# A hybrid decoder layer on one core: the tile of meta and decode tokens packed from 40 rows to 24

## The chip, the core and the metric

The kernel runs on one core of a Trainium2 chip. The metric is the device time in microseconds (us) of one execution. The engines are TensorE (PE, with its weight loads shown apart as PEld), VectorE (DVE), ScalarE (ACT), GpSimd (POOL) and SyncE (SP), which here only issues transfers. Each engine works through its own list in order and waits on semaphores for the others.

## The reference, cut to what matters

One layer of a decoder for 512 prompt tokens, 16 learned meta tokens in front of them and 8 decode tokens (one for each of 8 sequences). All is float32.

```python
p = rms_norm(x, g) @ w_in              # 1024 -> 3080: mq mk mv mo gates dq dk dv
# mLSTM heads (4) on mq, mk, mv, gates; differential attention heads (4) on dq, dk, dv;
# decode tokens: paged keys and values, and a kept state C, n, m
hm = rms_norm(h_m, g_m) * sigmoid(mo)
ha = rms_norm(a, g_da) * (1.0 - lam_init)
x = x + concatenate([hm, ha]) @ w_out  # 1024 -> 1024
# MoE: best of 4 groups, best 2 of its 8 experts (256 wide), SwiGLU, y summed with gates
for e in range(32):
    y += gates[:, e:e+1] * ((silu(h @ w_gate[e]) * (h @ w_up[e])) @ w_down[e])
```

## The kernel before, in words

Tokens lie in five tiles: tiles 0 to 3 hold 128 prompt tokens each, tile 4 (T4) the small rest. In T4 rows 0 to 15 are the meta tokens, rows 16 to 31 are padding and rows 32 to 39 are the decode tokens (S0 = 32, N4 = 40), so that each kind begins at a partition from which engines may start.

A list, `ORDER`, made by `schedule()`, sets the order in which all engines handle the items; each engine runs through the list and takes the part that is its own. Up to the experts it goes like this:

- The six projection blocks dv, dq, dk, mqk, mv, mo (512 columns each). An item `acc` (with `pre` as its first half) is a product for 128 or 512 prompt tokens; it runs 8 steps over the input dimension (L2054 where the result is stored by feature, L2057 where by token). An item `small` is the same block for T4 (L2071): the 40 rows of T4 are the weights of the array, the block's columns stream through. Since 40 rows fill less than half of the array's columns, the 512 columns of the block are cut in two halves of 256, whose results go to partitions 0 to 39 and 64 to 103 of one bank: two column groups of 64. ACT copies each half out (L1077).
- `qk`, `tp`, `pv` (attention of one tile and head: scores, turned weights, values) are woven between the products of blocks mqk, mv and mo, so that PE has work while DVE and ACT do the softmax. The decode tokens' attention is done beside it: `decscore`, `decsm`, `dect`, `decmix`, `decmix2` (L2010: values of four tokens at a time into four column groups of 32), `decsel`.
- The mLSTM: `decay`, `mqk_s`, `mpa`, `mpb` for four heads, `mdec1` to `mdec3` for the kept state of the decode tokens. `mdec1` needs the state C (`WS<-in_state_C`, L690) and the decode queries spread to all partitions (`DVt<-dec_mq`, L694), both brought by SP. Beside it `sig` items on DVE turn the gate mo of one half of a tile into a sigmoid times a gain (L1435, L1436, L1438).
- The output projection: `wa` (attention half, L2277) and `wo` (mLSTM half), each for tile and half of 512 columns, for T4 both halves together (L2281) in two column groups of 64. DVE adds the result to X (L1650, and for T4 also L1653). Norm (`hs`, `on`), turning (`ot`, `rt`), router (`logit`) lie around it.
- `rank`, `invert`, `order` find which rows go to which of 16 pairs of experts.

Then 17 turns over pairs of experts follow: gather of rows, gate and up (L2328), down (L2345), scatter. The 96 weight matrices of 1 MB are loaded by SP into 20 places; those for the first pairs are loaded as soon as a place is free, items 2 to 10 after `ot` of tile 0, for which SP waits until the product `wa` of T4 is done.

```python
ins = v.tensor_tensor(xs, xs, PS[b][0:n, :], ALU.add)          # wa, wo: L1650
...
drained(sp, ("pv",) + UNITS[-1], "p")                          # SP, item mdec1
```

## Time and profile before

| | us |
|---|---|
| median of 3 runs | 671.25 |
| lowest, highest | 669.18, 678.52 |
| the profiled execution, its own time | 677.67 |
| its span, first to last instruction | 675.8 |
| mean granted TensorE clock in it | 0.96 |

PE is busy for 91% of the span. The table of stretches below gives the busy time of each engine in one stretch, its instructions in brackets, then the granted clock of TensorE (1.00 is 2.4 GHz, 0.50 is 1.2 GHz), the busy share of the DMA engines and GB/s. In a timeline a row is: start in us, length in us, engine, line, operation, what it writes and reads, the size of the array used (rows*columns) or of the tiles, and in square brackets how long the engine stood still before it and who ended that. A float32 product counts as two instructions. The chain of waits is the chain of work that ended last, in order of time: start, length, what.

### The profile page before, as it was taken

What the parts mean: (1) busy time and instruction counts of PE and PEld (TensorE: products, weight loads), DVE (VectorE), ACT (ScalarE), POOL (GpSimd) and SP (SyncE); (2) the same over time, 40 slices, a digit from 0 to 9 for tenths busy, and PEclk for the clock granted to TensorE, in tenths of its full rate; (3) what the DMA queues carried; (4) which work ended last, traced back from release to release, by engine and by line L of the source; (5) the groups of instructions that cost most, each with busy time, mean ns of one, the idle gap of its engine ahead of it and who ended that gap; (6) DMA issues with size and microseconds to landing.
All of it is one profiled execution on the core that took longest, in us unless ns stands there. A gap on an engine that the chain in (4) does not pass through costs nothing.

```text
span 675.8 us, 8726 instructions
## 1 busy us (share of the span) xinstructions
PE 613.0 (91%) x3213; PEld 330.0 (49%) x3213; DVE 282.8 (42%) x637; ACT 139.7 (21%) x410; POOL 118.5 (18%) x206
## 2 busy tenths in 40 slices
PE   4999999799899999999989993899999996999792
PEld 2444444445544555555544562665555553555430
DVE  2320048443343434457969957714121221112066
ACT  2210132233332355221031110101001000100012
POOL 2341006220012011101032101111231111120013
PEclk9999999799999999999999896899999998999897
DMA  9636156750603030031759999599999999999993
GB/s 286 205 101 191 29 191 180 256 167 0 250 19 107 1 125 0 1 75 53 221 164 424 316 342 362 223 415 420 400 418 419 419 421 421 422 419 419 417 379 135
DMA packets 59409, 165.77 MB, mean 245 GB/s; under 512 B 18345, under 2 KB 27866, under 8 KB 46694
## 3 DMA queue, kind: packets, MB, share of 16 engines
q1 hardware_dynamic: 49590, 147.97, 57.6%
q0 software_dynamic: 7552, 17.19, 7.9%
q8 instruction: 27, 0.44, 0.3%
q10 hardware_dynamic: 2224, 0.04, 0.2%
q14 instruction: 16, 0.13, 0.1%
HBM read 150.88 MB, written 23.34 MB: 258 GB/s over the span
## 4 chain that ended last, share of the span: by engine, by line
PE 74%; DMA 13%; DVE 6%; ACT 2%; issue 2%; another core or an unknown queue 2%; POOL 0%; SPq 0%; POOLq 0%; DVEq 0%; ACTq 0%
PE bank L2054 12%; PE bank L2057 11%; PE bank L2277 9%; PE scores L2345 8%; PE bank_t L2328 6%; PE bank_p L2328 6%; DMA WS<-in_w_down_e 4%; DMA XHT<-in_w_down_e 4%; PE bank_t L2071 3%; PE bank L2318 2%; DMA WS<-in_w_in 2%; PE bank_p L2180 1%; PE scores L2197 1%; PE bank_t L2299 1%
## 5 line engine op out<-in xcount | busy, mean ns | idle before, releaser
L2057 PE MATMUL bank<-WS,XHT 128*128 128x512 f32 x192 | 89.1, 611 | 3.1 <-DMA WS<-in_w_in 2.6
L2054 PE MATMUL bank<-XHT,WS 128*128 128x512 f32 x192 | 86.5, 606 | 1.4 <-PE bank_t L2071 1.4
L2054 PEld LDWEIGHTS bank<-XHT,WS 128*128 128x128 f32 x192 | 36.3, 194 | 44.6 <-issue 44.3
L2057 PEld LDWEIGHTS bank<-WS,XHT 128*128 128x128 f32 x192 | 35.4, 193 | 44.7 <-issue 41.4
L2328 PE MATMUL bank_p<-WS,XHT 128*64 128x256 f32 x256 | 43.3, 381 | 1.5 <-DMA XHT<-in_w_up_e 1.3
L987 POOL DMA_INDIRECT out_rows<-MVA,slot_ids x15 | 15.1, 1008 | 153.1 <-DVE MVA L1851 150.4
L2328 PE MATMUL bank_t<-WS,XHT 128*64 128x256 f32 x224 | 39.4, 381 | 0.2 <-DVE XHT L1834 0.2
L874 POOL TENSOR_SCALAR rr<-ss 128x1 f32<-128x1 f32 (+3 forms) x25 | 7.3, 293 | 150.3 <-ACT XHT L1249 44.1
L2328 PEld LDWEIGHTS bank_p<-WS,XHT 128*64 128x64 f32 x256 | 26.8, 137 | 13.9 <-DMA XHT<-in_w_up_e 1.7
L2345 PE MATMUL scores<-WS,FT 128*64 128x512 f32 x72 | 28.0, 672 | 5.6 <-DMA WS<-in_w_down_e 5.6
L1851 DVE COPY MVA<-scores 128x512 f32<-128x512 f32 x16 | 11.1, 692 | 49.8 <-PE scores L2345 49.8
L2277 PE MATMUL bank<-WS,XHT 128*128 128x512 f32 x64 | 30.4, 623 | 0.0
L1586 DVE TENSOR_TENSOR scores<-scores,maskneg 128x256 f32<-128x256 f32 (+1 forms) x20 | 7.7, 383 | 54.3 <-PE scores L2151 49.2
L2277 PE MATMUL bank<-WS,FT 128*128 128x512 f32 x64 | 29.6, 605 | 0.1
L2328 PEld LDWEIGHTS bank_t<-WS,XHT 128*64 128x64 f32 x224 | 23.9, 137 | 11.2 <-issue 0.3
L1926 DVE TENSOR_TENSOR MVA<-DVt,bank_p 128x256 f32<-128x256 f32 x9 | 3.8, 421 | 59.6 <-ACT DVt L1292 59.6
L2328 PE MATMUL bank_p<-XHT 128*64 128x256 f32 x160 | 28.7, 381 | 0.0
L2328 PE MATMUL bank_t<-XHT 128*64 128x256 f32 x160 | 28.6, 381 | 0.0
L2318 PE MATMUL bank<-ident,DVt 128*128 128x128 f32 x136 | 20.5, 296 | 8.5 <-DMA DVt<-tok_rows,slot_ids 8.5
L915 POOL DMA_INDIRECT MO<-in_cache_k,pages x16 | 16.2, 1010 | 67.8 <-DVE before_mix L1540 50.4
L1077 ACT ACTIVATE MVA<-scores 128x512 f32<-128x512 f32 x18 | 10.6, 597 | 84.0 <-PE scores L2345 84.0
L1926 DVE TENSOR_TENSOR MVA<-DVt,bank_t 128x256 f32<-128x256 f32 x8 | 3.4, 421 | 52.6 <-ACT DVt L1292 52.6
(482 smaller groups left out, 1059.0 us busy)
## 6 DMA issues: line engine op xcount, KB each, us to landing
WS<-in_w_gate_e SPq DMA_DIRECT2D x16, 1024.0 KB, 8.8
WS<-in_w_up_e SPq DMA_DIRECT2D x14, 1024.0 KB
WS<-in_w_down_e SPq DMA_DIRECT2D x14, 1024.0 KB, 18.1
WS<-in_w_in SPq DMA_DIRECT2D x6, 2048.0 KB, 10.8
XHT<-in_w_up_e SPq DMA_DIRECT2D x10, 1024.0 KB
XHT<-in_w_down_e SPq DMA_DIRECT2D x9, 1024.0 KB, 21.4
XHT<-in_w_gate_e SPq DMA_DIRECT2D x8, 1024.0 KB, 30.3
FT<-in_w_up_e SPq DMA_DIRECT2D x6, 1024.0 KB
```

The costliest lines, as they stand in the source:

```text
L915: pool.indirect_dma_start(dst, None, cache[0].rearrange("n t h d -> (n t) (h d)"), bass.IndirectOffsetOnAxis(ap=pages[:, b * NPAGES + p:b ...
L987: pool.indirect_dma_start(end_rows if i in ENDING else out_rows, bass.IndirectOffsetOnAxis(ap=slot_ids[:, c, 1:2].bitcast(u32), axis=0), Y ...
L1077: return act.activation(dst, src, ACT.Copy, scale=scale)
L1586: link(v.tensor_tensor(diag, diag, maskneg[0:n, None, 0:n].to_broadcast([n, 2, n]), ALU.add))
L1851: v.tensor_copy(YO[s][:, 512:1024], Sps[:, 0, 512:1024]).then_inc(y1, 1)
L2054: mm = pe.matmul(PS[r][:, :], w[:, k, 128 * m:128 * (m + 1)], hT[:, k, 0:512], start=(k == 0), stop=(k == KC - 1))
L2057: mm = pe.matmul(PS[r][:, :], hT[:, k, 128 * m:128 * (m + 1)], w[:, k, :], start=(k == 0), stop=(k == KC - 1))
L2071: mm = pe.matmul(PS[r][64 * u:64 * u + N4, 0:256], hT[:, k, 512:TOK], w[:, k, 256 * u:256 * u + 256], start=(k == 0), stop=(k == KC - 1))
L2277: mm = pe.matmul(PS[b][0:n, :], rows[:, k, col(j):col(j) + n], blkslot[(6 + half) % 3][:, first + k, :], start=(k == 0), stop=(k == 3))
L2318: mm = pe.transpose(bank[k // 4][:, 128 * (k % 4):128 * (k % 4) + 128], src[:, k:D:KC], ident[:, :])
L2328: mm = pe.matmul(gu[64 * u:64 * u + 64, DE * g:DE * g + DE], rows[:, k, 64 * u:64 * u + 64], weights[kind, u][:, k, :], start=(k == 0), st ...
L2345: mm = pe.matmul(Sps[64 * u:64 * u + 64, 0, 512 * half:512 * half + 512], act_t[:, f, 64 * u:64 * u + 64], weights["down", u][:, f, 512 * ...
```

## The change

T4 is packed to 24 rows: the meta tokens in rows 0 to 15 and the decode tokens in rows 16 to 23 (SX = 16, NX = 24). With at most 32 rows a product of T4 fits a column group of 32. The `small` items of dv, dq, mqk, mv and mo now run in four column groups of 32, each over 128 of the block's columns; that of dk (the decode keys) stays in two groups of 64 over 256 columns. `wa` and `wo` of T4 run in four groups over 256 of the 1024 output columns each.

The part of the work that DVE, ACT and POOL do on decode tokens alone (rows 32 to 39) stays at those partitions. So five transfers issued by SP copy rows 16 to 23 of DVt, MQ4, MK, MVA and MO to rows 32 to 39, and `turned_rows` puts the turned rows back beside each other. The copy of MO needs the finished `sig` of T4, so the `sig` items come in the order of tiles 0, 1, T4, 2, 3; two more of them lie in the stretch of `mpa` 1 and `mqk_s` 2, two fewer in that of `wo` 2.

```diff
 TOK = SEQ + N4
+
+
+SX = NMETA
+NX = SX + NDEC
+ROWS = SEQ + NX
...
 def nrows(j):
+    return 128 if j < NT else NX
+
+
+def mixed_rows(j):
     return 128 if j < NT else N4
 
...
-    sig = iter([("sig", j, half) for j in range(NTILES) for half in range(2)])
+    sig = iter([("sig", j, half) for j in (0, 1, T4, 2, 3) for half in range(2)])
     gate = lambda: [next(sig)]
     norm = lambda kind: [(kind, j) for j in outer]
     order += [("decay", 0)] + more() + [("tp",) + prev, ("mqk_s", 0)] + more() + [("pv",) + prev] + norm("hsa")
     order += [("decay", 1), ("mpa", 0)] + gate() + more() + [("mqk_s", 1)] + norm("ona") + more() + [("mpb", 0), ("decay", 2)]
-    order += norm("oa") + gate() + more() + [("mpa", 1)] + gate() + more() + [("mqk_s", 2)] + gate() + more()
+    order += norm("oa") + gate() + gate() + more() + [("mpa", 1)] + gate() + gate() + more() + [("mqk_s", 2)] + gate() + more()
     order += [("mpb", 1), ("decay", 3), ("mdec1",)] + more() + [("mpa", 2)] + gate() + more() + [("mqk_s", 3), ("wsk",)] + more()
...
-        order += gate() if j == 2 else []
...
-        order += [("mdec3", 2), ("state",)] if j == 1 else gate() if j == 2 else []
+        order += [("mdec3", 2), ("state",)] if j == 1 else []
...
+def small_groups(b):
+
+    return 2 if b == "dk" else 4
...
+                        sp.dma_start(DVt[S0:N4, T4, :], DVt[SX:NX, T4, :]).then_inc(v_out, 16)
...
-                        sp.dma_start(dec_mq, MQ4[S0:N4]).then_inc(dm_out, 16)
-                        sp.dma_start(dec_mk, MK[S0:N4, T4, :]).then_inc(dm_out, 16)
+                        sp.dma_start(dec_mq, MQ4[SX:NX]).then_inc(dm_out, 16)
+                        sp.dma_start(dec_mk, MK[SX:NX, T4, :]).then_inc(dm_out, 16)
+                        sp.dma_start(MQ4[S0:N4], MQ4[SX:NX]).then_inc(dm_out, 16)
+                        sp.dma_start(MK[S0:N4, T4, :], MK[SX:NX, T4, :]).then_inc(dm_out, 16)
+                    elif item[1] == "mv":
+                        sp.dma_start(MVA[S0:N4, T4, :, 0:DV], MVA[SX:NX, T4, :, 0:DV]).then_inc(dm_out, 16)
+                elif item == ("sig", T4, 1):
+                    sp.wait_ge(mo_gated, 1)
+                    sp.wait_ge(dm_out, 16 * 5)
+                    sp.dma_start(MO[S0:N4, T4, :], MO[SX:NX, T4, :]).then_inc(dm_out, 16)
...
-                    sp.wait_ge(dm_out, 32)
+                    sp.wait_ge(dm_out, 16 * 5)
...
+            def turned_rows(dst, src, j):
+
+                src = src.rearrange("p (k t) -> p k t", t=128)
+                if j < NT:
+                    return copy(dst[:, 0:4, col(j):col(j) + 128], src)
+                copy(dst[:, 0:4, col(j):col(j) + NMETA], src[:, :, 0:NMETA])
+                return copy(dst[:, 0:4, col(j) + SX:col(j) + NX], src[:, :, S0:N4])
+
...
-                    for u in range(2):
-                        src = PS[r][64 * u:64 * u + N4, 0:256]
-                        cols = slice(256 * u, 256 * u + 256)
+                    groups = small_groups(b)
+                    for u in range(groups):
+                        src = PS[r][128 // groups * u:128 // groups * u + NX, 0:512 // groups]
+                        cols = slice(512 // groups * u, 512 // groups * (u + 1))
                         if b == "dq":
-                            ins = copy(tokst[0][0:N4, cols], src, DQ ** -0.5)
+                            ins = copy(tokst[0][0:NX, cols], src, DQ ** -0.5)
                         elif b == "dk":
-                            ins = copy(tokst[1][0:N4, cols], src)
+                            ins = copy(tokst[1][0:NX, cols], src)
                         elif b == "mqk":
-                            ins = copy(MK[0:N4, T4, :], src, DQ ** -0.5) if u else copy(MQ4, src)
+                            ins = (copy(MQ4[0:NX, cols], src) if u < 2 else
+                                   copy(MK[0:NX, T4, 128 * (u - 2):128 * (u - 1)], src, DQ ** -0.5))
                         elif b == "dv":
-                            ins = copy(DVt[0:N4, T4, cols], src)
...
+                    dve.wait_ge(dm_out, 16 * 5)
...
+                    if item == ("sig", T4, 1):
+                        v.nop().then_inc(mo_gated, 1)
...
+                    dve.wait_ge(v_out, 16 * 7)
...
+                        if j == T4:
+                            dve.wait_ge(dm_out, 16 * 6)
...
-                    xs = X[0:n, j, 512 * half:512 * half + 512]
-                    ins = v.tensor_tensor(xs, xs, PS[b][0:n, :], ALU.add)
+                    parts = [(slice(512 * half, 512 * half + 512), PS[b][0:n, :])]
                     if j == T4:
-                        xs = X[0:n, j, 512:1024]
-                        ins = v.tensor_tensor(xs, xs, PS[b][64:64 + n, :], ALU.add)
+                        parts = [(slice(256 * u, 256 * u + 256), PS[b][32 * u:32 * u + n, 0:256]) for u in range(4)]
+                    for c, product in parts:
+                        ins = v.tensor_tensor(X[0:n, j, c], X[0:n, j, c], product, ALU.add)
                     ins.then_inc(freed[b], 1)
...
+                    groups = small_groups(b)
+                    rows, cols = 128 // groups, 512 // groups
                     for k in range(KC):
-                        for u in range(2):
-                            mm = pe.matmul(PS[r][64 * u:64 * u + N4, 0:256], hT[:, k, 512:TOK],
-                                           w[:, k, 256 * u:256 * u + 256], start=(k == 0), stop=(k == KC - 1))
+                        for u in range(groups):
+                            mm = pe.matmul(PS[r][rows * u:rows * u + NX, 0:cols], hT[:, k, 512:ROWS],
+                                           w[:, k, cols * u:cols * u + cols], start=(k == 0), stop=(k == KC - 1))
...
-                        for u in range(2):
-                            mm = pe.matmul(PS[b][64 * u:64 * u + n, :], rows[:, k, 512:TOK], blkslot[(6 + u) % 3][:, first + k, :],
+                        for u in range(4):
+                            mm = pe.matmul(PS[b][32 * u:32 * u + n, 0:256], rows[:, k, 512:ROWS],
+                                           blkslot[(6 + u // 2) % 3][:, first + k, 256 * (u % 2):256 * (u % 2) + 256],
                                            start=(k == 0), stop=(k == 3))
```

DVE, from the end of item `mpa` of head 1 to the beginning of `mpb` of head 1, before (L1435, L1436, L1438 are one `sig` item, L1650 adds a product `wa` to X, L1601 to L1605 multiply scores):

```order
L1622 TENSOR_TENSOR XHT<-bank_t,den 128x3x128 [waits dve_step]
L1435 TENSOR_SCALAR MO<-MO 128x256 [waits freed_a1,freed_t]
L1436 RECIPROCAL MO<-MO 128x256 [waits dve_step]
L1438 TENSOR_TENSOR MO<-MO,head_gains 128x256 [waits dve_step]
L1650 TENSOR_TENSOR XHT<-XHT,bank 128x512 [waits filled_a0,dve_step]
L1601 TENSOR_TENSOR WS<-WS,scores 128x896 [waits filled_Sa,decay_masked]
...
L1435 TENSOR_SCALAR MO<-MO 128x256 [waits freed_a1]
```

and in the changed program (L1469, L1470, L1472 are the `sig` item, L1692 is the addition, L1638 the scores):

```order
L1659 TENSOR_TENSOR XHT<-bank_t,den 128x3x128 [waits dve_step]
L1469 TENSOR_SCALAR MO<-MO 128x256 [waits freed_a1,freed_t]
L1470 RECIPROCAL MO<-MO 128x256 [waits dve_step]
L1472 TENSOR_TENSOR MO<-MO,head_gains 128x256 [waits dve_step]
L1469 TENSOR_SCALAR MO<-MO 24x256 [waits freed_a0,dve_step]
L1470 RECIPROCAL MO<-MO 24x256 [waits dve_step]
L1472 TENSOR_TENSOR MO<-MO,head_gains 24x256 [waits dve_step]
L1692 TENSOR_TENSOR XHT<-XHT,bank 128x512 [waits filled_a0,dve_step]
L1638 TENSOR_TENSOR WS<-WS,scores 128x896 [waits filled_Sa,decay_masked]
...
L1469 TENSOR_SCALAR MO<-MO 24x256 [waits freed_a0]
```

Between the end of `mpa` 1 and the scores there are two `sig` items where there was one, and both `sig` items of T4 now stand here; the other half of tile 1 stands ahead of `mpa` 1, right behind the last item of tile 0.

SP, from the load of the last weight block to the spreading of the decode queries, before:

```order
L599 DMA WS<-in_w_out 128x8x512 [waits block_used]
L690 DMA WS<-in_state_C 128x32x64 [waits block_used,freed_a0,freed_t]
L694 DMA DVt<-dec_mq 128x2048 [waits v_out,freed_p,dm_out]
L697 DMA dec_w<-dr 8x4 [waits dw_made]
L698 DMA dec_w<-dr 8x4
```

and in the changed program:

```order
L612 DMA WS<-in_w_out 128x8x512 [waits block_used]
L678 DMA MVA<-MVA 8x4x128 [waits freed_t]
L682 DMA MO<-MO 8x512 [waits dm_out,mo_gated,freed_a0]
L711 DMA WS<-in_state_C 128x32x64 [waits block_used]
L715 DMA DVt<-dec_mq 128x2048 [waits v_out,freed_p,dm_out]
L718 DMA dec_w<-dr 8x4 [waits dw_made]
```

The copy of MO, which waits for the last `sig` item of T4 on DVE (`mo_gated`), stands ahead of the two transfers that `mdec1` on DVE waits for.

## Rows read from the trace of the kernel before

**Rows 1.** Page, part 1: busy us, share of the span and instructions.
```profile
PE 613.0 (91%) x3213; PEld 330.0 (49%) x3213; DVE 282.8 (42%) x637; ACT 139.7 (21%) x410; POOL 118.5 (18%) x206
```
**Rows 2.** Table of stretches: busy time by engine, clock, DMA share, GB/s.
```profile
126.00:136.00 10.00, 9.14 (x37) 5.15 (x35) 1.88 (x12) 4.00 (x12) 0.17 (x1) 0.66 0.72 271
...
293.00:350.00 57.00, 56.57 (x226) 29.17 (x226) 43.57 (x102) 10.26 (x41) 6.83 (x15) 1.00 0.46 133
...
413.00:440.00 27.00, 16.50 (x131) 12.10 (x133) 19.30 (x69) 2.58 (x7) 4.23 (x4) 0.74 0.69 275
440.00:540.00 100.00, 100.00 (x748) 56.95 (x746) 23.49 (x56) 10.04 (x24) 21.02 (x26) 1.00 1.02 415
```
**Rows 3.** Chain of waits: start, length, what.
```profile
213.15 2.03 PE bank_p L2010 x16
...
346.83 3.59 PE bank L2281 x16
...
353.21 0.66 PE scores L2260 x4
```
**Rows 4.** Timeline of PE in `decmix2`, four column groups of 32.
```profile
213.08 0.63 PE L2010 MATMUL bank_p<-MO,Wd 128*32 128x512 f32 x2
...
213.53 0.61 PE L2010 MATMUL bank_p<-MO,Wd 128*32 128x512 f32 x2
```
**Rows 5.** Timeline of PE: two runs of short products, then `small` of mo.
```profile
86.25 0.74 PE L2037 MATMUL bank_p<-XHT,wg 128*36 128x40 f32 x16
...
292.91 3.65 PE L2071 MATMUL bank<-WS,XHT 128*40 128x256 f32 x32
...
410.90 0.70 PE L1999 MATMUL bank_t<-MO 128*64 128x8 bf16 x20 [1.74 <-DVE MO L1728]
```
**Rows 6.** Timeline around `small` of dq (ACT) and of mqk.
```profile
81.06 0.77 ACT L1077 ACTIVATE XHT<-bank_t 40x256 f32<-40x256 f32 x2 [3.00 <-PE bank_t L2071]
...
158.44 0.25 ACT L1077 ACTIVATE WS<-scores 16x128 f32<-16x128 f32 x1
...
166.84 0.37 DVE L1594 SCALAR_TENSOR_TENSOR WS<-WS,sums 128x144 f32<-128x144 f32 x1
...
168.82 0.27 PE L2161 MATMUL scores<-ident,WS 128*16 128x128 f32 x1
```
**Rows 7.** Timeline of DVE from `mpb` 0 to `wo` of T4.
```profile
294.20 0.29 DVE L1435 TENSOR_SCALAR MO<-MO 128x256 f32<-128x256 f32 x1
...
296.32 0.43 DVE L1438 TENSOR_TENSOR MO<-MO,head_gains 128x256 f32<-128x256 f32 x1
300.20 0.16 DVE L1618 SCALAR_TENSOR_TENSOR den<-bank_t,RC 128x3 f32<-128x3 f32 x1 [3.46 <-PE bank_t L2220]
...
305.53 1.09 DVE L1601 TENSOR_TENSOR WS<-WS,scores 128x896 f32<-128x896 f32 x1 [0.88 <-PE scores L2197]
307.12 0.55 DVE L1603 TENSOR_TENSOR WS<-WS,scores 128x384 f32<-128x384 f32 x1 [0.51 <-PE scores L2201]
...
312.38 0.16 DVE L1618 SCALAR_TENSOR_TENSOR den<-bank_p,RC 128x1 f32<-128x1 f32 x1 [0.86 <-PE bank_p L2220]
...
320.21 2.29 DVE L1392 TENSOR_TENSOR DVt<-DVt,WS 128x2048 f32<-128x2048 f32 x1
...
325.22 0.68 DVE L1650 TENSOR_TENSOR XHT<-XHT,bank 128x512 f32<-128x512 f32 x1
...
398.25 0.68 DVE L1650 TENSOR_TENSOR XHT<-XHT,bank 40x512 f32<-40x512 f32 x1 [1.63 <-PE bank L2281]
```
**Rows 8.** Transfers issued from 293 to 325 us: size, us to landing.
```profile
DVt<-dec_mq SPq DMA_DIRECT2D x1, 1024.0 KB, 9.0
...
WS<-in_state_C SPq DMA_DIRECT2D x1, 0.2 KB, 7.4
```
**Rows 9.** Chain of waits, later rows: the first gather, the last pairs.
```profile
413.07 7.91 DMA DVt<-tok_rows,slot_ids
...
542.11 29.82 DMA WS<-in_w_down_e
```

More of the change, by code:

```diff
@@ L46 @@
 SECOND = 1024
-assert TOK <= SECOND
+assert ROWS <= SECOND
 NPAIRS = GROWS // 128
@@ L502, in build @@
         gfew, pwfew = few[:, 0:64], few[:, 64:66]
-        pick, alike = tri[0:N4, :], maskneg
+        pick, alike = tri[0:NX, :], maskneg
         left = [place[i % PLACES] for i in range(len(READ) - PLACES, len(READ) - PLACES + 6)]
@@ L710, in _ @@
                         for rows in (out_rows, end_rows):
-                            sp.dma_start(spread(rows, SECOND * c + SEQ + S0), maskneg[:, 0:64]).then_inc(rows_zeroed, 16)
+                            sp.dma_start(spread(rows, SECOND * c + SEQ + SX), maskneg[:, 0:64]).then_inc(rows_zeroed, 16)
                 elif kind == "state":
@@ L800, in _ @@
             further(sp, more, further_pair, stored=all_out)
-            sp.dma_start(XE[T4], spread(x_rows, SEQ + S0)).then_inc(x_back[T4], 16)
+            sp.dma_start(XE[T4], spread(x_rows, SEQ + SX)).then_inc(x_back[T4], 16)
             for i in range(len(READ) - PLACES, len(READ) - PLACES + 6):
@@ L817, in _ @@
                 for c in range(2):
-                    sp.dma_start(Yfew[:, 2 * n + c], spread(rows, SECOND * c + SEQ + S0)).then_inc(y_in[T4], 16)
+                    sp.dma_start(Yfew[:, 2 * n + c], spread(rows, SECOND * c + SEQ + SX)).then_inc(y_in[T4], 16)
             done = 0
@@ L832, in _ @@
             sp.wait_ge(tok_out, 16 * 6)
-            sp.wait_ge(v_out, 16 * 6)
+            sp.wait_ge(v_out, 16 * 7)
         @block.gpsimd
@@ L1084, in _ @@
                     after(act, item, "p")
-                    act.activation(rI[:, 0:N4], PS["p"][0:H, 0:N4], ACT.Identity, bias=bgi[:, :])
+                    small_columns = ((slice(0, NMETA), slice(0, NMETA)), (slice(S0, N4), slice(SX, NX)))
+                    for dst, src in small_columns:
+                        act.activation(rI[:, dst], PS["p"][0:H, src], ACT.Identity, bias=bgi[:, :])
                     for u in range(2):
@@ L1089, in _ @@
                                        ACT.Identity, bias=bgi[:, :])
-                    act.activation(rF[:, 0:N4], PS["p"][32:32 + H, 0:N4], ACT.Identity, bias=bgf[:, :]).then_inc(freed["p"], 1)
+                    for dst, src in small_columns:
+                        ins = act.activation(rF[:, dst], PS["p"][32:32 + H, src], ACT.Identity, bias=bgf[:, :])
+                    ins.then_inc(freed["p"], 1)
                     act.activation(rF[:, N4:N4 + 256], PS["t"][32:32 + H, 0:256], ACT.Identity, bias=bgf[:, :])
@@ L2036, in _ @@
                     for k in range(KC):
-                        mm = pe.matmul(PS["p"][0:36, 0:N4], wg[:, k, :], hT[:, k, 512:TOK], start=(k == 0), stop=(k == KC - 1))
+                        mm = pe.matmul(PS["p"][0:36, 0:NX], wg[:, k, :], hT[:, k, 512:ROWS], start=(k == 0), stop=(k == KC - 1))
                     mm.then_inc(filled["p"], 1)
@@ L2377, in _ @@
                     pe.wait_ge(sel_made, 2)
-                    pe.matmul(Sps[:, 1, 0:2], pick, pw[0:N4, :, T4], start=True, stop=True).then_inc(few_filled, 1)
+                    pe.matmul(Sps[:, 1, 0:2], pick, pw[0:NX, :, T4], start=True, stop=True).then_inc(few_filled, 1)
                 if i == 0:
```

76 lines of the change are left out of this document (37 added, 39 removed).

## The prediction

> **What bounds the kernel now.** I began with the busy shares: PE is at work for 91% of the span [rows 1], so time taken from PE is wanted, but only where PE ends last. The table of stretches says where that is [rows 2]. From 293 to 350 us PE is busy for 56.57 of 57 us, while DVE already has 43.57. From 440 us on the DMA engines are full (share 1.02, 415 GB/s), and late in the experts the chain stands for 29.82 us on down weights [rows 9]: that phase has a length that transfers set, and only its start can move. It begins with the first gather, 7.91 us after its request [rows 9], in a stretch whose DMA share is 0.69 with loads that were queued earlier. So the change is worth what it takes from PE up to about 413 us, less what DVE or a transfer gives back.
>
> **Price of a product in four groups.** A `small` block costs 3.6 us: 32 instructions in 3.65 with the last one's tail [rows 5], 113 ns each. `wa` and `wo` of T4 cost 3.59 for 16 [rows 3]. `decmix2` is the nearest row for four groups: 16 instructions over 512 columns in 2.03 us [rows 3], rounds of four beginning at 213.08 and 213.53 [rows 4]. A round lasts 0.45 us at most, about what one such instruction streams (2 passes x 512 columns at 2.4 GHz = 0.427), and a quarter of it is each one's share. With 128 columns that gives 107/4 = 27 ns each, 64 x 27 = 1.7 us; with 256 columns 53 ns, 32 x 53 = 1.7 us. What may forbid the 27 ns is issue or the change of weights. The rows nearest are runs of very short products: 16 in 0.74 us and 20 in 0.70 [rows 5], which after a tail of 0.15 to 0.2 are 28 to 36 ns each. So a block takes 1.7 to 2.3 us; I take 1.9, the middle, since a round of `decmix2` is a few per cent over its streaming. **A block saves 1.7 (1.2 to 1.9), `wa` or `wo` of T4 saves 1.8 (1.6 to 1.9).**
>
> A rule of the Trainium skill speaks against this. The page "TensorE: Matmul & The Clock Gate" (Measured speedup vs the span model) gives 3.07 for four tiles of the array at once (of rows, those of columns near them), not 4. By it a block would be 16 x 0.427 / 3.07 = 2.2 us, the saving 1.4, and the sum below about 1.1 us smaller in its first four blocks. `decmix2` shows 16 x 0.427 / 2.03 = 3.4 with its tail, and I follow the row.
>
> **Part by part.**
> - dv: the products of other blocks follow directly on PE. 1.7.
> - dq: the transposes behind it wait for ACT, which copies two pieces of 256 columns in 0.77 us; the small copies nearby take 0.25 each [rows 6], so four take 1.0. 1.7 - 0.2 = 1.5.
> - dk stays in two groups: 0.
> - mqk: attention is woven in. A turn at 168.82 needs scores that DVE ends at 166.84 + 0.37 = 167.21 [rows 6]; so 1.6 of the gain fit before PE waits. 1.6.
> - mv: 1.7. Ahead of 293 us that makes 6.5.
> - mo and `wa` of T4 lie in the stretch where DVE is the closest rival. PE gains 1.7 at 292.91 [rows 5]. DVE now has two `sig` items ahead of `mpa` 1; one costs 296.32 + 0.43 - 294.20 = 2.55 us. The second fits into the idle 3.46 ahead of 300.20, less the 1.7 that PE comes earlier, but not wholly: DVE is then 0.8 earlier than before, not 1.7 [rows 7]. Behind `mpa` 1 the next extra `sig` (2.55; 24 rows are no cheaper, since the columns decide) eats the idle 0.88, 0.51 and 0.86 [rows 7]. DVE comes to the decode product (320.21) at 320.21 - 0.8 - 2.25 + 2.55 = 319.7.
> - The new wait: SP copies MO only when `sig` of T4 is done, and behind that copy, in the same queue, stand the loads of C and of the spread queries. In this clock that `sig` ends 1.5 us ahead of the old `den` at 312.38 less the gains, near 311.2, so the loads go out at 311.5 to 312.4. The queries took 9.0 us to land, C 7.4 [rows 8]: landed at 321.4. DVE waits 1.7 us for them, and everything behind it on DVE with it: the addition of `wa` at 325.22 [rows 7] comes at about 326.4, and frees the bank that PE wants for `wa` 2. PE is 1.2 late there where it had been 1.7 early.
> - `wa` of T4 then gives 1.8, and DVE behind it has four additions of 256 columns for two of 512: 4 x 0.46 against 2 x 0.69 (0.42 is the price of 256 columns, from the `sig` product of 0.43 [rows 7], 0.04 a step), +0.45. `ot` 1 at 353.21 [rows 3] comes at 353.21 + 1.2 - 1.8 + 0.45 = 353.1. The whole stretch, mo and `wa` together, is worth **0.1, not 3.5**. Were the loads early enough it would be worth 1.9; were they 2 us later, it would cost 1.9.
> - `wo` of T4: the chain goes from PE through DVE, which waits 1.63 for it [rows 7]. 1.8 on PE less 0.3 on DVE (a turn follows while the last additions run): 1.5.
> - The five copies are of 8 rows, and no engine but SP waits in front of them; the extra wait of `mdec1` is for copies of blocks that are done before its own inputs. The turned rows of T4, two copies for one on ACT, lie beside PE. 0.
>
> Sum: 6.5 + 0.1 + 1.5 = 8.1 us on the path to the gather. The weight loads ahead of the gather are released by `wa` of T4, which moves by 6.5 + 0.6; since the gather lands behind them [rows 9], it gains between 7.1 and 8.1. **I take 7.5.** The profiled execution (677.67 us, 6.4 above the median) would be 670.2; against the median, 671.25 - 7.5 = 663.8 us, 1.1% less.
>
> **Rivals.**
> 1. *The forecast*, chance 0.5: 664 us, 661 to 666.
> 2. *Everything counts.* The loads come in time, 5 x 1.8 + 2 x 1.8 = 12.6 us, giving 658.7; and if the stretch from 126 to 136 with a granted clock of 0.66 [rows 2] runs at full speed once the work has moved, 3.4 more: 655.3. For it: DVE idles 13 us in 293 to 350, and another order of transfers may land the queries faster than 9.0. Against it: the wait on `sig` is in the program. Chance 0.17.
> 3. *The gain is taken back.* The delay in DVE's stretch is 2 us larger, mqk or the softmax makes PE wait for DVE, the gather stays behind weight loads whose start moved little. Then 2 to 5 us remain: 666 to 669. For it: PE's gain arrives piecewise among waits of under 1 us. Also a clock dip in a new place would do this: half speed over 3.4 us costs 1.7. Chance 0.27.
> 4. *Slower: the four groups don't overlap at short length.* If an instruction keeps its 113 ns because issue or weight change takes it, 5 x 64 + 2 x 32 = 384 instructions take 43.4 us in place of 7 x 3.6 = 25.2: 671.25 + 18.2 = 689 us. It decides from 25.2/384 = 66 ns on; over 2% slower from 100 ns. Against it: 28 to 36 ns in two runs [rows 5]. Those are not in four groups with 128 columns, so not nothing. Chance 0.06, of it 0.04 over 2%; a price just under 66 ns would leave the time where it is, 670 to 671, and has 0.02 of it.
>
> A sharper form of the last stands in the same page of the Trainium skill (Wait — 56ns, not 53.3ns?): with hardware decode off a MATMUL costs the sequencer about 62 ns. A block would then take 64 x 62 = 4.0 us, longer than now, and only `wa` and `wo` would gain: some 670 us. The runs at 28 to 36 ns [rows 5] exclude that here, if instructions of those products count alike.
>
> **How the numbers follow.** The predicted time is that of rival 1. The range 657 to 670 leaves out the part of rival 2 with the clock, some of rival 3 that gives nothing, and rival 4, together under 0.2. About 2% is what a measurement can tell from no change (the three runs shown lie 9 us apart), 13.4 us here: faster by more needs under 657.8, part of rival 2, 0.08; slower by more needs over 684.7, 0.04; the rest is 0.88.
>
> **What would show it.** A `small` block of 64 instructions near 1.9 us and `wa` of T4 near 1.8; above 3.6 rival 4 is on. DVE's idle ahead of the multiplication by C should be ended by the load of the queries and last 1 to 2 us, with PE standing before `wa` 2; if there is none, rival 2. `ot` 1 should come 6 to 7 us earlier than before, the first gather 7 to 8, and the time from the gather to the end should be unchanged: if that grows, rival 3. I am wrong in the mechanism if PE's gain ahead of 293 us is under 5 us.

## The result, and the profile after

| | before | changed |
|---|---|---|
| median of 20 runs, us | 673.44 | 669.75 |
| lowest, highest | 669.18, 678.52 | 663.67, 674.59 |
| the profiled execution, its own time, us | 677.67 | 673.30 |

The ratio is 0.9931 (95% interval 0.9911 to 0.9951), and 0.9929 (0.990 to 0.996) when the same kernel ran again: together 0.9930 +- 0.0017, 4.7 +- 1.2 us (the two medians in the table lie 3.7 us apart). The ratios leave out single executions with a lower clock and over 1.5% above the fastest, of the changed kernel's 20 the one at 674.59. The forecast was 7.5 us. The sign and the order are right, the size is not: some 60% of it came by the ratio, half by the medians.

The first part of the profile's page, and the table of stretches, for the changed kernel:

```profile
PE 607.1 (90%) x3405; PEld 331.2 (49%) x3405; DVE 283.0 (42%) x642; ACT 141.3 (21%) x424; POOL 121.0 (18%) x205
```
```profile
126.00:136.00 10.00, 8.60 (x31) 3.60 (x30) 4.61 (x23) 3.78 (x20) 2.61 (x3) 1.00 0.81 261
...
293.00:350.00 57.00, 52.52 (x205) 27.34 (x204) 45.96 (x104) 9.24 (x42) 8.41 (x14) 0.95 0.54 162
...
413.00:440.00 27.00, 22.88 (x173) 16.09 (x175) 16.04 (x50) 2.44 (x4) 1.98 (x2) 0.83 0.68 268
440.00:540.00 100.00, 100.00 (x736) 55.77 (x734) 24.09 (x57) 10.66 (x26) 21.06 (x26) 1.00 1.02 416
```

Set against [rows 2]: PE has lost its full load in 293 to 350 us (52.52 of 57, it was 56.57), DVE has a little more. The stretch from 126 us now has full clock, that from 293 has not: 0.95.

The timeline of PE shows the new products, and the way through the mLSTM:

```profile
74.94 1.95 PE L2112 MATMUL bank_t<-WS,XHT 128*24 128x128 f32 x64
...
284.23 1.95 PE L2112 MATMUL bank<-WS,XHT 128*24 128x128 f32 x64
287.10 0.46 PE L2259 MATMUL bank_t<-MVA,WS 128*128 128x129 f32 x2 [0.93 <-ACT FT L1097]
...
291.20 6.02 PE L2318 MATMUL bank<-WS,FT 128*128 128x512 f32 x8
...
321.56 3.67 PE L2318 MATMUL bank<-WS,FT 128*128 128x512 f32 x8 [2.13 <-DVE XHT L1692]
...
342.28 1.93 PE L2322 MATMUL bank<-WS,FT 128*24 128x256 f32 x32
...
347.76 1.12 PE L2301 MATMUL scores<-ident,XHT 128*128 128x128 f32 x4 [2.28 <-DVE XHT L1682]
```

A block of 64 instructions takes 1.95 us with its tail, where it had 3.65 for 32 [rows 5]; `wa` of T4 takes 1.93. Ahead of `wa` 2 PE stands for 2.13 us. At 291.20 eight instructions that take 3.7 us elsewhere take 6.02: TensorE is at its lower level of clock there (granted clock 0.63 in 290 to 298 us).

Two of the signs that the prediction named can be read here. PE comes to mo 8.7 us earlier (284.23, it was 292.91), where 6.5 was forecast; this one pair flatters the change, since the trace of before has half clock at 126 to 136 us. `ot` 1 comes 5.45 us earlier (347.76, it was 353.21 [rows 3]), where 6 to 7 was forecast.

DVE in the same stretch:

```profile
303.85 0.41 DVE L1472 TENSOR_TENSOR MO<-MO,head_gains 24x256 f32<-24x256 f32 x1
...
315.73 2.29 DVE L1426 TENSOR_TENSOR DVt<-DVt,WS 128x2048 f32<-128x2048 f32 x1 [1.88 <-DMA DVt<-dec_mq]
...
344.68 1.69 DVE L1692 TENSOR_TENSOR XHT<-XHT,bank 24x256 f32<-24x256 f32 x4
```

The first row is the end of the `sig` of T4, the second the product with C, which waits for the spread queries; it had no wait before [rows 7]. The third is the four additions of `wa` of T4. And SP's own timeline (start, the time that the issue takes, what):

```profile
304.39 0.68 SPq L682 DMA_DIRECT2D MO<-MO  x1
305.64 0.83 SPq L711 DMA_DIRECT2D WS<-in_state_C  x1
306.60 3.62 SPq L715 DMA_DIRECT2D DVt<-dec_mq  x1
```

The copy of MO goes out at the moment the `sig` is done (303.85 + 0.41 = 304.26), and the queries 2.2 us after the copy, since each of the two issues ahead takes SP 0.7 to 0.8 us and there is a gap of 0.57 behind the copy.

In the chain of waits, later rows:

```profile
390.34 1.90 PE bank L2322 x32
...
407.32 7.86 DMA DVt<-tok_rows,slot_ids
```

The first gather is asked for 5.75 us earlier than before (413.07, [rows 9]), and lands as long after.

### The profile page after: what moved, and what is told of

The parts are those of the page before. It is cut to its first block, busy times and chain, and to the rows that moved or that the text cites. A ratio compares the mean times of both kernels' runs of the same rounds, so it can differ in the third digit from the quotient of the medians.

```text
span 671.5 us, 9135 instructions
## 1 busy us (share of the span) xinstructions
PE 607.1 (90%) x3405; PEld 331.2 (49%) x3405; DVE 283.0 (42%) x642; ACT 141.3 (21%) x424; POOL 121.0 (18%) x205
## 4 chain that ended last, share of the span: by engine, by line
PE 61%; DMA 16%; DVE 9%; issue 7%; ACT 4%; POOL 2%; another core or an unknown queue 1%; SPq 0%; POOLq 0%; DVEq 0%; ACTq 0%
PE bank L2096 11%; PE scores L2387 8%; PE bank L2093 7%; PE bank_t L2370 6%; PE bank_p L2370 6%; PE bank L2318 5%; DMA XHT<-in_w_down_e 5%; DMA WS<-in_w_down_e 5%; DMA MO<-in_cache_k,pages 2%; PE bank L2360 2%; DMA WS<-in_w_in 2%; PE bank_p L2221 1%; PE bank_t L2341 1%; PE scores L2189 1%; DMA DVt<-tok_rows,slot_ids 1%
## 5 line engine op out<-in xcount | busy, mean ns | idle before, releaser
L2093 PE MATMUL bank<-XHT,WS 128*128 128x512 f32 x192 | 85.0, 597 | 0.6 <-PE bank_t L2112 0.3
L2096 PEld LDWEIGHTS bank<-WS,XHT 128*128 128x128 f32 x192 | 35.5, 193 | 43.9 <-issue 41.4
L2318 PE MATMUL bank<-WS,FT 128*128 128x512 f32 x64 | 31.9, 644 | 2.1 <-DVE XHT L1692 2.1
```

Source lines behind the costliest of these rows:

```text
L2093: mm = pe.matmul(PS[r][:, :], w[:, k, 128 * m:128 * (m + 1)], hT[:, k, 0:512], start=(k == 0), stop=(k == KC - 1))
L2096: mm = pe.matmul(PS[r][:, :], hT[:, k, 128 * m:128 * (m + 1)], w[:, k, :], start=(k == 0), stop=(k == KC - 1))
L2318: mm = pe.matmul(PS[b][0:n, :], rows[:, k, col(j):col(j) + n], blkslot[(6 + half) % 3][:, first + k, :], start=(k == 0), stop=(k == 3))
```

## The experiments

Unless another thing is said, a gain or loss in us against the kernel before is one minus the ratio, times 674. "Half clock" is the lower level of TensorE's granted clock.

**The same kernel again**, for its ratio.

> The changed kernel once more, unaltered, for a second trace. In the first trace TensorE's granted clock was at half from about 290 to 297 us and at 205 to 207, where the kernel before had full clock, and at full clock at 126 to 136, where the kernel before was at 0.66. Theory A (the dips lie where the order of the work puts them): the second trace has them in the same places, and the ratio is again near 0.993. Theory B (the dips fall anywhere): the 290 us dip is gone or elsewhere, and the profiled run, if free of dips before 350 us, is 3 us shorter than 673.3, near 670. Both expect the 1.9 us blocks and DVE's wait of 1.9 us for the spread queries to be there.

Measured: ratio 0.9929. The profiled execution was the longest of its ten (680.36 us against a median of 671.52), so its own places of half clock decide little. The later traces of kernels near to it say more: full clock at 126 to 136 us in most, half clock somewhere in 160 to 212 us in most, and, in eleven of all twenty traces, again at `ot` 1 (beginning at 339 to 354 us). Neither theory holds as it stood: the places are few, and which of them is hit changes from trace to trace.

**Packing alone.**

```diff
 def small_groups(b):
-    return 2 if b == "dk" else 4
+    return 2
...
-                        parts = [(slice(256 * u, 256 * u + 256), PS[b][32 * u:32 * u + n, 0:256]) for u in range(4)]
+                        parts = [(slice(512 * u, 512 * u + 512), PS[b][64 * u:64 * u + n, :]) for u in range(2)]
...
-                        for u in range(4):
-                            mm = pe.matmul(PS[b][32 * u:32 * u + n, 0:256], rows[:, k, 512:ROWS],
...
+                        for u in range(2):
+                            mm = pe.matmul(PS[b][64 * u:64 * u + n, :], rows[:, k, 512:ROWS], blkslot[(6 + u) % 3][:, first + k, :],
```

> Everything of the change but the four groups: T4 has 24 rows, the copies and the new order of the sig items stand, and the products of T4 are in two column groups of 64 as before. Theory (packing is paid for in DVE's stretch): DVE has no 1.7 us from PE ahead of mpa 1, so it comes to the product with C at about +0.3 us against the kernel before and waits about 1.7 us for the spread queries: 1.5 to 2.5 us slower than before, ratio 1.003. Rival (packing is free, what is missing of the gain is lost elsewhere): ratio 1.000, within 0.5 us, and no wait for the queries.

Measured: 1.0050 (1.0017 to 1.0084), 3.4 us slower than before. DVE's row and PE's `wa` 2 in its trace:

```profile
322.55 2.29 DVE L1425 TENSOR_TENSOR DVt<-DVt,WS 128x2048 f32<-128x2048 f32 x1 [2.68 <-DMA DVt<-dec_mq]
```
```profile
328.38 5.37 PE L2317 MATMUL bank<-WS,FT 128*128 128x512 f32 x8 [2.94 <-DVE XHT L1691]
```

The wait is 2.68 us, not 1.7, and behind PE's stop of 2.94 us eight instructions take 5.37 us and not 3.67: half clock, 1.7 us more. Against the trace of before, PE is 0.5 us early ahead of the stop, 2.3 late at `wa` 2 and 4.0 late after it, and nothing later gives it back up to the gather.

**The copy of MO behind the two loads.** The one edit that moves the result most, run four times. SP issues the copy after the loads of C and of the queries.

```diff
-                elif item == ("sig", T4, 1):
-                    sp.wait_ge(mo_gated, 1)
-                    sp.wait_ge(dm_out, 16 * 5)
-                    sp.dma_start(MO[S0:N4, T4, :], MO[SX:NX, T4, :]).then_inc(dm_out, 16)
...
                     sp.dma_start(QB, dec_mq.rearrange("b n -> (b n)").partition_broadcast(128)
                                  .rearrange("p (b d) -> p b d", d=DQ)).then_inc(qb_in, 16)
+                    sp.wait_ge(mo_gated, 1)
+                    sp.dma_start(MO[S0:N4, T4, :], MO[SX:NX, T4, :]).then_inc(dm_out, 16)
```

> The changed kernel with one edit: SP issues the copy of MO behind the loads of C and of the spread queries, not ahead of them. Theory (the queue order costs the wait): DVE's wait of 1.88 us for the queries goes, the additions behind it come 1.9 us earlier and wa 2 on PE no longer waits its 2.13 us; 1 to 2 us faster than the changed kernel, ratio to before 0.990 to 0.9915. Rival (the front part doesn't set the end, or the stretch is bound by DVE's own work): the wait is gone in the trace, but the first gather moves by less than 0.5 us and the ratio stays at 0.993.

> The kernel with the copy of MO behind the loads once more, for its ratio (0.985, 0.980 to 0.990, rests on six runs) and a second trace. Theory (wait and what follows it cost about 5 us): ratio again 0.984 to 0.988. Rival (the first was lucky in its clock, the wait costs its 1.9 us): 0.989 to 0.991.

> The kernel with the copy behind once more, beside the others on one chip. Its two ratios, 0.985 and 0.984, rest on six and five runs. Expected 0.984 to 0.986; if it is 0.988 or more, the copy's place is worth the 2.7 us of DVE's wait and no more.

> The kernel with the copy behind and mqk in four groups, on the same chip as the two others, so that all three stand beside each other: expected 0.985 to 0.988, mean clock 0.960.

Measured: 0.9850, 0.9838, 0.9890 and 0.9876; weighted 0.9870 +- 0.0019, 8.8 +- 1.3 us faster than before and 4.0 +- 1.7 us faster than the changed kernel. The four intervals overlap (0.9855 to 0.989); the first two ratios rest on six and five runs and lie lowest, and the third, at 0.989, missed what was expected of it and spoke for 2.7 us as the price of the copy's place, which 4.0 +- 1.7 leaves open. SP in the first trace, and PE ahead of `wa` 2 in the second:

```profile
290.89 4.71 SPq L711 DMA_DIRECT2D DVt<-dec_mq  x1
304.19 0.73 SPq L714 DMA_DIRECT2D MO<-MO  x1
```
```profile
316.82 3.67 PE L2316 MATMUL bank<-WS,FT 128*128 128x512 f32 x8 [0.29 <-DVE XHT L1690]
```

The queries go out 13 us ahead of the copy, DVE doesn't wait for them, and PE's stop is 0.29 us. The stretch from the beginning of mo to `ot` 1 takes 58.4 us in all eight traces with the copy behind and `wa` of T4 in four groups (58.38 to 58.41); these are its ends in the first:

```profile
286.12 1.95 PE L2110 MATMUL bank<-WS,XHT 128*24 128x128 f32 x64
...
344.53 0.66 PE L2299 MATMUL scores<-ident,XHT 128*128 128x128 f32 x4 [2.29 <-DVE XHT L1680]
```

Before it took 60.3 us (292.91 to 353.21), in the changed kernel's two traces 63.5 and 63.7.

**The same on packing alone.**

> Packing alone (two column groups throughout) with the copy of MO behind the two loads. Theory (of the cost of packing alone, 3.4 us, the queue order is most): near the kernel before, ratio 0.999 to 1.001, no wait for the queries. Rival (the sig items and the other copies cost): still 1.003 to 1.005.

Measured: 0.9994 (0.9961 to 1.0026). The theory held: packing costs nothing that can be measured (0.4 +- 2.2 us faster), and moving one copy takes back what packing alone had lost (3.8 +- 3.1 us of 3.4 +- 2.3). In the traces the stretch from mo to `ot` 1 takes 64.8 us with the copy ahead and 60.4 with it behind, 0.1 more than before.

**Copy behind, and two `sig` items ahead of `mpa` 0.**

```diff
-    order += [("decay", 1), ("mpa", 0)] + gate() + more() + ...
-    order += norm("oa") + gate() + gate() + more() + [("mpa", 1)] + gate() + gate() + more() + ...
+    order += [("decay", 1)] + gate() + gate() + [("mpa", 0)] + gate() + more() + ...
+    order += norm("oa") + gate() + more() + [("mpa", 1)] + gate() + more() + ...
```

> As the one before, and besides two sig items are moved from behind mpb 0 and mpa 1 to ahead of mpa 0, where DVE stood idle for 7 us in the kernel before. Theory: DVE's stretch from 290 to 320 us gets back to its old load, so that PE keeps the 1.7 us of mo as well: DVE's wait and the second delay are gone, 3 us faster than the changed kernel, ratio to before 0.988 to 0.9895. Rival (only the queue mattered): the same as with the copy behind alone. Second rival (clock): the gain depends on whether the half clock at 290 us stays.

Measured: 0.9893 (0.9857 to 0.9930), no better than the copy behind alone. The ratio lies in the theory's range, but that range was set against 0.990 or more for the copy behind, which came out at 0.9870. PE goes from mo to `ot` 1 in 58.4 us in both traces, 1.9 less than before. Only the queue mattered; DVE's two more `sig` items cost PE nothing.

**`wa` and `wo` of T4 in two groups, copy behind.** The edit of the copy, and of packing alone the hunks on `wa` and `wo`.

> The changed kernel with the copy behind the loads, and wa and wo of T4 in two column groups of 64 over 512 columns: only the small blocks are in four. By the terms of the sum wa and wo are worth 1.35 and 1.5 us on the path: 2.9 us slower than the kernel with the copy behind and wa, wo in four; ratio to before 0.989 to 0.990. Rival (the gains of wa and wo are met by DVE's four additions and by the weight loads): within 1 us of it, ratio 0.985 to 0.986.

Measured: 0.9875 (0.9826 to 0.9924) against the 0.9870: inconclusive by time. In the traces the two products are worth 1.0 us (`wa`: mo to `ot` 1 takes 59.4 us here) and 1.7 us (`wo`, between 378 and 398), together the 2.7 that my sum had as 2.9. Why so little of it is seen in the time may lie at `ot` 1:

```profile
344.08 0.66 PE L2299 MATMUL scores<-ident,XHT 128*128 128x128 f32 x4 [1.82 <-DVE XHT L1680]
```

With `wa` of T4 in two groups PE stands 1.82 or 1.83 us there, in all six traces of it, and none has half clock at that place. With four groups DVE has four additions for two, the stop is 2.27 to 2.29 us in all fourteen traces, and in eleven of them half clock begins within 1.3 us of its end. It makes the way from `ot` 1 to `wo` 1.5 us longer (42.9 us against 41.4, and 41.2 against 39.7), more than the 1.0 that four groups give `wa`. Whether the longer stop does it, and whether `wa` in two groups beside `wo` in four is the better kernel, wasn't tried.

**PE's stop filled with work.** Products whose result nobody reads, ahead of `wa` 2, on the changed kernel and on packing alone: five of them, in the two later kernels three.

```diff
+                    if item == ("wa", 2, 0):
+                        before(pe, ("mpb", 2), "p")
+                        for again in range(5):
+                            pe.matmul(PS["p"][:, :], dqT[:, 0, 0:128], blkslot[0][:, 4, :], start=True, stop=True)
                     before(pe, item, b)
```

> The changed kernel with five products added on PE (2.1 us at full clock, into a bank that nobody reads) ahead of wa 2, where PE stands for 2.13 us because DVE is late with the queries' wait. They compute nothing that is used. Theory (the wait costs more than its length: PE's stop is followed by half clock, as at 324 us in the second trace and in the one with packing alone): the wait is still there, on DVE, but the clock from 320 to 340 us is full and the time is 1.5 to 3 us shorter than the changed kernel, ratio 0.989 to 0.991. Rival (the clock falls by itself): ratio 0.993 to 0.994, since the added work fits the wait and changes nothing, and half clock is found in 320 to 340 as often as without.

> Packing alone (two column groups, the copy of MO ahead of the loads), with the same five products of 2.1 us on PE ahead of wa 2. With packing alone DVE waited 2.68 us for the queries, PE was 2.8 us later at wa 2, and half clock at 328 us made that 4.5; the ratio was 1.005, and 0.9994 with the copy behind. Theory (a stop of PE of this length brings half clock with it): the DVE wait stays, the stop is filled, no half clock in 320 to 345 us, ratio 1.002 to 1.0035. Rival (no tie between the stop and the clock): ratio 1.005 or a little over, for the filling takes 2.1 us and gives nothing.

> The changed kernel with the stop ahead of wa 2 filled, once more: the first gave 0.9896 with an interval of 0.984 to 0.996 from five undisturbed runs, which tells nothing apart. Theory: 0.989 to 0.991. Rival: 0.993.

> Packing alone, copy ahead, with three products ahead of wa 2 in place of five. In the trace of the kernel with five, these took 4.4 us (ten instructions of 0.44), not the 2.1 I had put down, where the stop to be filled was 2.94 us: wa 2 came 1.4 us later than without filling, and yet the ratio was the same (1.0052 and 1.0050), the mean clock back from 0.961 to 0.966. Three take 2.6 us and fit into the stop. Theory (the stop of PE brings half clock, worth 1.7 us or more): ratio 1.0025 to 1.0035, mean clock near 0.965. Rival (the clock isn't tied to the stop): 1.005.

> The changed kernel with three products (2.6 us) ahead of wa 2, where PE stands 2.1 to 3.2 us. Theory: no half clock in 320 to 345 us, ratio 0.990 to 0.991. Rival: 0.993, and half clock there as often as without the filling.

I had put five products down as 2.1 us, and they take 4.4, for a float32 product is two instructions of 0.44. PE with packing alone and five of them:

```profile
324.44 4.56 PE L2317 MATMUL bank_p<-WS,FT 128*128 128x512 f32 x10
328.84 3.60 PE L2321 MATMUL bank<-WS,FT 128*128 128x512 f32 x8
```

Measured, with the mean granted clock of the runs:

| | ratio | mean clock |
|---|---|---|
| changed, stop open (two runs of it) | 0.9930 +- 0.0017 | 0.959 |
| changed, five products (two) | 0.9896, 0.9923 | 0.962, 0.961 |
| changed, three products | 0.9921 | 0.960 |
| packing alone, stop open | 1.0050 +- 0.0034 | 0.961 |
| packing alone, five | 1.0052 +- 0.0034 | 0.966 |
| packing alone, three | 1.0029 +- 0.0032 | 0.966 |
| packing alone, copy behind (no stop) | 0.9994 +- 0.0033 | 0.965 |
| before | 1 | 0.964 to 0.966 |

In five traces with the stop filled none has half clock right behind it; of four with it open three have (packing alone, the changed kernel's second trace, and the one with mqk in two below), each losing 1.7 us or more. In the two-group kernel the mean clock comes back in full, in the changed kernel it doesn't. The time of the whole kernel says less: 1.4 +- 3.1 us won with three products in packing alone, 0.8 +- 1.9 in the changed kernel with all three fillings together. Of the five ratios two lie in the range that the theory gave (0.9896 and 1.0029), the other three above it, towards the rival's number or at it. So that half clock follows this stop is shown by the traces; that its removal shortens the kernel is not shown.

The fillings with three products show one thing more. They fit into the stop: `wa` 2 still waits for DVE, and the clock is full. So these traces have the price of the wait by itself:

```profile
283.29 1.95 PE L2112 MATMUL bank<-WS,XHT 128*24 128x128 f32 x64
...
318.36 3.70 PE L2322 MATMUL bank<-WS,FT 128*128 128x512 f32 x8 [0.37 <-DVE XHT L1692]
...
344.58 0.66 PE L2301 MATMUL scores<-ident,XHT 128*128 128x128 f32 x4 [2.28 <-DVE XHT L1682]
```

From mo to `ot` 1 that is 61.3 us, 2.9 more than the 58.4 with the copy behind. In packing alone it is 63.3 against 60.4, 2.9 again. With the stop open and half clock behind it the same stretch takes 63.2 and 63.7 us in four groups, 64.8 in packing alone: 1.4 to 2.5 us more, which is the clock.

**The block mqk back in two groups.**

```diff
-    return 2 if b == "dk" else 4
+    return 2 if b in ("dk", "mqk") else 4
...
-                            ins = (copy(MQ4[0:NX, cols], src) if u < 2 else
...
+                            ins = copy(MK[0:NX, T4, :], src, DQ ** -0.5) if u else copy(MQ4[0:NX], src)
```

> The kernel with the copy behind the loads, the block mqk back in two column groups. With all five-group blocks the traces show half clock for 3 to 7 us somewhere in 160 to 212 us, and the mean clock of the runs is 0.960 to 0.961, where the two-group kernel with the copy behind has none there and 0.965. Theory (four-group mqk is what brings it): clock back to 0.963 or more, the 1.7 us of the block lost, 2 to 3 us won: ratio 0.983 to 0.985. Rival (mqk has no part in it): the 1.6 us of my sum are lost, ratio 0.987, mean clock 0.961.

> The changed kernel with one edit: the block mqk in two column groups again, the copy of MO left ahead of the loads. With the copy behind, the same edit brought the mean clock from 0.960 to 0.9655 and cost no time. Theory (mqk in four groups costs in clock what it gives in streaming): ratio 0.992 to 0.994, mean clock 0.962 to 0.964 (the stop of PE ahead of wa 2 keeps its share). Rival (the block is worth its 1.6 us): ratio 0.9955, mean clock 0.960.

> The fastest kernel so far by its ratio (0.9855 from six runs) once more: mqk in two groups, copy behind. Expected 0.984 to 0.988 with a mean clock of 0.965; with 0.989 or more it is no better than all blocks but dk in four groups, whose three ratios are 0.985, 0.984 and 0.989.

Measured: with the copy behind 0.9855 and 0.9873, weighted 0.9865 +- 0.0027, mean clock 0.964: the same as with mqk in four (0.9870, 0.960). With the copy ahead 0.9958 (0.9932 to 0.9983), mean clock 0.958 as with mqk in four: 1.9 +- 2.1 us slower than with mqk in four, where the block was forecast at 1.6; both numbers are the rival's. The stretches 155 to 215 us of two traces, mqk in two and in four, copy behind:

```profile
155.00:215.00 60.00, 55.86 (x288) 30.46 (x289) 21.27 (x53) 20.40 (x70) 7.60 (x8) 1.00 0.31 106
```
```profile
155.00:215.00 60.00, 55.11 (x310) 31.04 (x310) 19.88 (x51) 20.52 (x70) 7.57 (x8) 0.94 0.31 106
```

Of twelve traces with mqk in four groups eleven are below full clock in this stretch, of eight with it in two three are. So with the copy behind the block in four groups shows no gain in time (in two it is 0.3 +- 2.2 us faster), and clock may be part of why; the pair with the copy ahead speaks against it. Open.

The kernel with mqk in two and the copy ahead also has the longest stop ahead of `wa` 2 of all traces, and half clock behind it:

```profile
316.99 5.35 PE L2317 MATMUL bank<-WS,FT 128*128 128x512 f32 x8 [3.41 <-DVE XHT L1691]
```

**dk in four groups as well, copy behind.**

```diff
-    return 2 if b == "dk" else 4
+    return 4
```

> The kernel with the copy behind the loads, and the block of the decode keys in four groups as well. Its 3.64 us become 1.95 on PE. Behind it PE goes on with the block mqk, and then waits for ACT's copies of these keys (0.43 us ahead of the turns at 119 us). Theory (the block is on PE's path): 1.2 to 1.7 us faster, ratio 0.982 to 0.983 where the kernel without it has 0.9845. Rival (ACT's copies and the transfers of the keys set the turns): the same within 0.5 us.

Measured: 0.9941 (0.9910 to 0.9972), 4.8 +- 2.5 us slower than with dk in two. Both theories fell. PE and ACT around it:

```profile
111.20 1.93 PE L2110 MATMUL bank_t<-WS,XHT 128*24 128x128 f32 x60
113.36 0.42 PE L2110 MATMUL bank_t<-WS,XHT 128*24 128x128 f32 x4 [0.23 <-issue]
118.79 2.05 PE L2091 MATMUL bank<-XHT,WS 128*128 128x512 f32 x2 [5.00 <-remote]
```
```profile
118.52 1.11 ACT L1095 ACTIVATE XHT<-bank_t 24x128 f32<-24x128 f32 x4 [6.62 <-remote]
```

The block does take its 1.9 us, but then PE and ACT both stand until 118.5, released by nothing that the profile can name, and half clock follows to 122.5 us. In the program both wait there for the signal of the block's last product. The ratio and the low mean clock of all twelve runs (0.957) say that this kernel is slower; that each of them has this stop isn't shown, for one was traced.

Nor is the stop shown to come from the four groups. Packing alone, with dk in two groups, has one at the same place:

```profile
119.97 5.37 PE L2092 MATMUL bank<-XHT,WS 128*128 128x512 f32 x8 [2.08 <-remote]
```

ACT stood for 4.75 us ahead of that. And in the trace of before ACT stood for 5.23 us up to 125.04, released in the same way, and PE 2.13 us for ACT; the half clock at 126 to 136 us [rows 2] comes right behind it. What holds these engines stays open.

## Why the prediction was wrong in size

The table puts the steps against what they measured.

| step | forecast | measured |
|---|---|---|
| a block in four groups | 1.9 us | 1.95 with its tail |
| PE's gain at the beginning of mo | 6.5 us | 8.7 in the first pair, 7.3 on average (11 traces against 5) |
| mo to `ot` 1, loads in time | 1.9 us | 1.9 (copy behind) |
| `wa`, `wo` of T4 | 1.8 saved each, 1.35 and 1.5 on the path | 1.0 and 1.7 |
| five blocks, `wa` and `wo`, no wait for the queries | 7.5 + 1.8 = 9.3 us | 8.8 +- 1.3 (copy behind) |
| packing itself | 0 | 0.4 +- 2.2 faster |
| DVE's wait for the queries | 1.7 us | 1.88, and 2.7 to 3.5 in eight other traces |
| what the copy's place costs, by the ratios | 1.8 us | 4.0 +- 1.7 in four groups, 3.8 +- 3.1 in two |
| the same, mo to `ot` 1 in the traces | 1.8 us | 2.9 at full clock, 4.4 to 5.3 as it ran |
| gather | 7.5 earlier | 5.8 earlier in the first pair |
| from the second turn's first gate and up product to the end | unchanged | 241.3 us on average of 15, against 239.8 of 5 |

**Right:** the price per instruction. `decmix2` and the short products [rows 3 to 5] gave 27 to 36 ns, and 1.92/64 is 30. By the Trainium skill's page "TensorE: Matmul & The Clock Gate" (Measured speedup vs the span model) the 3.07 that it gives for four row tiles would have made 2.2 us; the trace gives 16 x 0.427 / 1.92 = 3.6, and the measurement decides. The same page's 62 ns per MATMUL with hardware decode off (Wait — 56ns, not 53.3ns?) isn't met here: 30 ns. Right too was the place where the change gives back: the queue of SP, DVE's product with C, `wa` 2 on PE. The waits stand where the prediction put them.

**The step that failed** is the term on the wait: the new wait for the spread queries, which the sum has at 1.8 us (0.1 instead of 1.9 for the stretch of mo and `wa`). The mechanism was right and the size was not. I wrote that the loads go out at 311.5 to 312.4, with the `sig` done at 311.2, 0.3 us for the copy and 0.9 for the load of C. SP takes 0.68 and 0.83 us for these issues and has a gap of 0.57 between them: the queries go out 2.3 us after the `sig`, not 1.2. That is 1.1 us more of wait on DVE and PE, and 1.8 + 1.1 = 2.9 is what the two traces at full clock show. The 0.9 for the load of C could be read in SP's own timeline of before, where issues have a length:

```profile
297.52 0.79 SPq L690 DMA_DIRECT2D WS<-in_state_C  x1
298.41 3.78 SPq L694 DMA_DIRECT2D DVt<-dec_mq  x1
```

The copy itself had no row there; 0.3 is the low end of the small issues in that trace (0.26 to 0.60 us), and it took 0.68 and the gap. Behind it PE's stop of 2.1 to 3.4 us, which the prediction counted by its length, brought 1.7 us or more of half clock in three traces of four. 1.8 + 1.1 + 1.3 = 4.2 agrees with the 4.0 +- 1.7 that the place of the copy measures.

That DVE's wait in the first trace, 1.88 us, is so near to the 1.7 of the forecast is luck. There DVE comes to the product with C 9.6 us after the `sig`, because it waits for PE, which half clock at 290 us had made late; in three later traces (the same again, five products once more, mqk in two) it comes 8.4 us after it, and the wait is 2.9 to 3.1 us.

**Taken as fixed and not quite so:** the experts. I let the gain pass whole through a phase that transfers bind. In 15 traces with blocks in four groups the phase, from the second turn on, is 241.3 us long on average (240.1 to 243.1), in the five without 239.8 (238.2 to 240.7). So 1.5 +- 0.9 us of the gain is given back there; why wasn't tried. It need not be the groups: of the five, the one that comes there earliest (packing alone, copy behind) has the longest phase.

**Terms that were wrong and cancelled.** With the loads in time mo and `wa` of T4 give the 1.9 us of the forecast, and that is luck. The prediction had 0.5 for mo, by way of DVE, and 1.35 for `wa`; the traces give 0.9 to 1.1 and 1.0. Of the 1.7 that mo saves on PE 0.6 goes to a wait for ACT (0.93 us, it was 0.32), and DVE's extra `sig` items, charged with 0.9 and 0.3 us, cost PE nothing once the queries are in time (the kernel with them ahead of `mpa` 0). Ahead of mo the gain was 0.8 us larger than forecast on average, but single traces lie up to 9 us apart there, by their clock. And half clock at `ot` 1, 1.5 us in eleven traces of fourteen, was in no term: 1.2 on average.

7.5 + 0.8 - 1.1 - 1.3 - 1.2 - 1.5 = 3.2, against 4.7 +- 1.2. Each of these terms is an average over few traces and known to 1 us or so; the sum shows that they are of the right order, and doesn't prove each.

Rival 2 (everything counts) would have needed the queries in time: the copy behind the loads is that kernel, and it reached 8.8, not 12.6. Rival 4 was excluded by the first block. Rival 3 is where the measured 4.7 us lies (2 to 5 us), and two of the ways that it named came about: a larger delay in DVE's stretch and half clock in a new place.

## What to carry to other kernels

- A transfer that is put ahead of others in a queue costs them its wait and the time of its issue, and that of each one between. Read SP's own timeline, and add the issues; moving one copy of 16 KB behind two loads was worth about as much as the change itself (4.0 +- 1.7 against 4.7 +- 1.2 us).
- Price a packed product from the nearest packed product in the same trace, not from a general factor: `decmix2` said 27 ns, and it was 30.
- A stop of TensorE of 2 to 3 us may cost more than its length. Look at the duration of the eight instructions behind it, not at the stop alone.
- To price a wait, compare one stretch between two fixed instructions of PE in several traces, and those at full clock by themselves: here it repeats to 0.03 us, where the time of the whole kernel is known to 1 or 2 us.

The fastest version here is the change with the copy of MO behind the loads of C and the queries: 0.9870 +- 0.0019, with mqk in two groups or in four.

## What the hardware showed that was not expected

- The mean level of TensorE's clock changes from run to run of one program: the changed kernel's 20 runs go from 663.67 us at a mean granted clock of 0.970 to 674.59 at 0.950. Kernels with blocks in four column groups have a mean of 0.957 to 0.963, and once 0.966 (mqk in two, copy behind; 0.962 when it ran again); packing alone has 0.961 with PE's stop open. The kernel before and packing alone without an open stop have 0.964 to 0.966.
- Half clock often comes right behind a stop of PE, but not each time, and not only there. At 202 to 209 us nine of the 20 traces have it, and in all nine PE had just stood for 1.57 to 1.74 us; two had such a stop and kept full clock, and none whose longest stop there was 1.03 us or less has it. At 164 to 175 us eleven have it without a stop of 0.9 us ahead.
- Weights of 24 columns in four groups with 128 streamed columns reach 30 ns an instruction, 3.6 times as fast as the estimate of 0.427 us for each 512 columns one after another.
- Somewhere in 112 to 125 us ACT stood still for 4.7 to 6.6 us, released by "remote", in the traces of three quite different kernels (before, packing alone, dk in four groups), and PE for 2 to 5 us with it.
